# Two convolutions placed anew, and two matrix stages that start on finished tiles

## What is computed

```python
h = rmsnorm_2(x, g_mix[l])
z = h @ w_in[l]
za = z[..., : 2 * D_A] + b_glu[l]
zb = z[..., 2 * D_A: 2 * D_A + D_B]
zc = z[..., 2 * D_A + D_B:]
ua = za[..., :D_A] * jax.nn.sigmoid(za[..., D_A:])
va = causal_dwconv(ua, w_dw_a[l]) + b_dw_a[l]
va = jax.nn.silu(layernorm(va, ln_g_a[l], ln_b_a[l]))
ya = va @ w_a_out[l]
yb = multiscale_pool(zb, w_pool_grp[l], pool_scale[l]) @ w_b_out[l]
gb, gc, xv = zc[..., :D_C], zc[..., D_C: 2 * D_C], zc[..., 2 * D_C:]
yc = (gb * causal_dwconv(gc * xv, w_dw_c[l])) @ w_c_out[l]
gates = jax.nn.sigmoid(h @ w_gate[l] + b_gate[l]).reshape(b, s, N_BRANCH, d)
merged = gates[:, :, 0] * ya + gates[:, :, 1] * yb + gates[:, :, 2] * yc
x = x + merged @ w_o[l]
h2 = rmsnorm_2(x, g_mlp[l])
x = x + jnp.square(jax.nn.relu(h2 @ w_up[l])) @ w_down[l]
```

## Time and profile before

| | us |
|---|---|
| median of 3 runs | 3545.73 |
| lowest, highest | 3545.4, 3550.69 |
| the profiled execution, its own time | 3549.25 |
| its span, first to last instruction | 3547.5 |
| TensorE busy | 3401.6 (96%) |
| VectorE busy | 2297.2 (65%) |
| ScalarE busy | 1234.8 (35%) |
| GpSimd busy | 530.2 (15%) |
| mean granted TensorE clock | 0.979 |

### The profile page before, as it was taken

One profiled execution on the slowest core, in us unless ns is written; L12 is line 12 of the kernel. 1 busy time (PEld: TensorE's weight loads), 2 busy tenths in 40 slices (PEclk: granted clock), 3 DMA queues, 4 the chain that ended last, 5 costly groups with the idle time before them and its releaser, 6 DMA issues.

```text
span 3547.5 us, 71271 instructions
## 1 busy us (share of the span) xinstructions
PE 3401.6 (96%) x31330; PEld 2955.4 (83%) x31330; DVE 2297.2 (65%) x2408; ACT 1234.8 (35%) x1125; POOL 530.2 (15%) x307
## 2 busy tenths in 40 slices
PE   7999799899999999999999998999999999999998
PEld 4777568798888988898889886888888878888887
DVE  7684144699998964796479655449747556564444
ACT  2000142344443334333433333343443334343332
POOL 0374000000354520252035200020000000000000
PEclk8999899999999999999999999999999999999999
DMA  9656594355444555445544553554545545555553
GB/s 412 240 231 278 219 393 168 143 191 202 179 177 180 189 192 209 172 185 199 204 180 180 187 193 140 190 208 172 213 171 197 191 148 195 203 199 190 196 206 119
DMA packets 52019, 713.18 MB, mean 201 GB/s; under 512 B 5690, under 2 KB 7754, under 8 KB 8848
## 3 DMA queue, kind: packets, MB, share of 16 engines
q1 hardware_dynamic: 48528, 700.47, 52.5%
q0 software_dynamic: 1136, 8.17, 0.6%
q10 hardware_dynamic: 2192, 2.10, 0.2%
HBM read 707.04 MB, written 3.67 MB: 200 GB/s over the span
## 4 chain that ended last, share of the span: by engine, by line
PE 87%; DVE 8%; DMA 4%; ACT 1%; issue 1%; DVEq 0%; SPq 0%; ACTq 0%
PE psW L477 24%; PE psW L478 24%; PE psW L479 24%; PE psW L475 6%; DVE ring L982 3%; DMA ring<-wst_dram 3%; DVE arena L1563 2%; PE psM L505 1%; PE psW L545 1%; DMA h_act<-bias_rows 1%; PE psM L699 1%; PE psM L527 1%; PE psM L545 1%; DVE proj L1441 1%; DVE work L1339 1%
## 5 line engine op out<-in xcount | busy, mean ns | idle before, releaser
L982 DVE SCALAR_TENSOR_TENSOR ring<-ring 128x2048 f16<-128x2048 f32 x526 | 1276.7, 2468 | 541.7 <-ACT ring L1688 541.3
L477 PE MATMUL psW<-h_act,ring 128*128 128x256 f16 x5088 | 1391.6, 274 | 49.0 <-DVE h_act L1331 16.6
L478 PE MATMUL psW<-h_act,ring 128*128 128x256 f16 x5088 | 1391.6, 274 | 0.0
L479 PE MATMUL psW<-h_act,ring 128*128 128x256 f16 x5088 | 1391.5, 273 | 0.0
L1688 ACT ACTIVATE ring<-ring 128x2048 f16<-128x2048 f32 x526 | 974.7, 1903 | 862.1 <-PE psW L479 809.2
L477 PE MATMUL psW<-arena,ring 128*128 128x256 f16 x3072 | 841.3, 274 | 8.4 <-DVE arena L1454 4.3
L478 PE MATMUL psW<-arena,ring 128*128 128x256 f16 x3072 | 841.4, 274 | 0.0
L479 PE MATMUL psW<-arena,ring 128*128 128x256 f16 x3072 | 841.2, 274 | 0.0
L477 PEld LDWEIGHTS psW<-h_act,ring 128*128 128x128 f16 x5088 | 498.7, 98 | 125.2 <-issue 40.5
L479 PEld LDWEIGHTS psW<-h_act,ring 128*128 128x128 f16 x5088 | 499.5, 98 | 59.2
L478 PEld LDWEIGHTS psW<-h_act,ring 128*128 128x128 f16 x5088 | 498.9, 98 | 57.9
(11 more groups left out here) (340 smaller groups left out, 2411.9 us busy)
## 6 DMA issues: line engine op xcount, KB each, us to landing
ring<-wst_dram SPq DMA_DIRECT2D x333, 2048.0 KB, 7.8
x_res<-xT_dram POOLq DMA_DIRECT2D x2, 2048.0 KB, 17.4
out_dram<-x_res SPq DMA_DIRECT2D x4, 512.0 KB, 2.6
bias_rows<-proj POOLq DMA_DIRECT2D x1, 1536.0 KB, 21.9
x_res<-cmat_dram POOLq DMA_DIRECT2D x1, 1024.0 KB, 6.7
x_res<-bmat_dram ACTq DMA_DIRECT2D x8, 128.0 KB, 2.6
h_act<-bias_rows ACTq DMA_DIRECT2D x1, 1024.0 KB, 32.2
dyn<-dyn_dram POOLq DMA_DIRECT2D x1, 480.0 KB, 23.6
```

What stands on the lines that cost most here:

```text
L477: nc.tensor.matmul(out, whi(s, col, P), xh, start=first, stop=False)
L478: nc.tensor.matmul(out, whi(s, col, P), xl, start=False, stop=False)
L479: return nc.tensor.matmul(out, wlo(s, col, P), xh, start=False, stop=last)
L982: ins = stt(wlo(s, c, n), ring[:, s * UNIT + c:s * UNIT + c + n], WSCALE, whi(s, c, n), ALU.mult, ALU.subtract)
```

## The change

It does five things.

1. The short convolution becomes a generator of its own, `short_branch()`, and its pieces run ahead of `low` in z's units 11 to 15 (16 is empty).
2. The long convolution yields every two taps, so it takes the pieces 0 to 14 of the gate stage; one empty piece follows, and the layer norm starts at piece 16 as before.
3. Gate uses bank (j + 1) % 4, abc begins with `psM`, w_o uses bank (j + 3) % 4 with `lead=3`, and gate, abc, w_o and down are entered without draining.
4. `merged` is counted up by each abc unit (from 1), and w_o's first unit waits ahead of every second k for the tiles that it reads. The wait of `merge` for VectorE's own last instruction becomes one on `merged`.
5. down starts once `relu_sb` has counted 16 units, and asks for all 32 behind its first unit. The first turn (four units) of w_o and of down is now written out.

```diff
+            from_h1 = lambda s, j: unit_a(s, (j + 1) % 4, h_split)
+            stage("gate", from_h1, n=16, drained=False)
...
-                ps = psW if j % 2 == 0 else psM
+                ps = psM if j % 2 == 0 else psW
...
-            stage("abc", abc, lead=3)
-            pe_.wait_ge(merged, 1)
-            stage("w_o", from_h)
+            stage("abc", abc, lead=3, drained=False)
+            def w_o_head(s, j):
+                for m in range(2):
+                    for k in range(KT):
+                        if m == 0 and k % 2 == 0:
+                            pe_.wait_ge(merged, k // 2 + 2)
+                        mm = product(psW[:, 3, m * T:(m + 1) * T], s, k * 256 + m * P, h_split(k), k == 0, k == KT - 1)
+                return mm
+            stage("w_o", lambda s, j: unit_a(s, (j + 3) % 4, h_split), lead=3, head=w_o_head, drained=False)
...
-            pe_.wait_ge(relu_sb, 32 + 4)
-            stage_sums("down", lambda s, j: unit_b(s, j, lambda k: halves(A, k)), 8)
+            def down_head(s, j):
+                mm = down(s, j)
+                pe_.wait_ge(relu_sb, 4 + 32)
+                return mm
+            pe_.wait_ge(relu_sb, 4 + 16)
+            stage("down", down, n=24, lead=2, drained=False, head=down_head)
...
+            def short_branch():
+                v.wait_ge(bank_free, FIRST["z"] + 9 + 4)
+                step(tt(tiles(J, 6, 6), tiles(J, 6, 6), tiles(J, 12, 6), ALU.mult))
+                for k in range(6):
+                    D.put(ts(tiles(J, 12 + k), tiles(J, 6 + k), const("w_dw_c", 3 * k + 2), None, ALU.mult))
+                yield
...
+                if n >= 11:
+                    next(short)
                 low(FIRST["z"] + n + 2)
...
-                    if tap % 3 == 0:
+                    if tap % 2 == 0:
                         yield
...
-                D.wait()
+                v.wait_ge(merged, i * 4 + (j + 1))
...
-                D.put(tt(hl[:, :, 1, :], w, hl[:, :, 0, :], ALU.subtract))
-            lows("abc", merge, 24)
-            D.wait()
-            v.sem_inc(merged, 1)
+                tt(hl[:, :, 1, :], w, hl[:, :, 0, :], ALU.subtract).then_inc(merged, 1)
+            lows("abc", merge, 20)
```

## The result

| | before | after |
|---|---|---|
| median, lowest to highest (5 runs each) | 3545.73 (3543.44 to 3550.69) | 3527.12 (3521.49 to 3529.23) |
| span of the profiled execution | 3547.5 | 3525.4 |
| mean granted clock | 0.979 | 0.980 |

A forecast was written before the change was run, and what follows sets the result against it. TensorE, busy 96% of the span, was taken as the bound, so only its standstills and slow clock could be won. 1.38 + 7.01 + 1.48 + 6.7 + 6.11 = 22.7 us gave median 3523.0; own range 3519.5 to 3526, full range to 3529.

The forecast's parts named there:

- rival (1): Bare entries to gate, abc, w_o and down cost 1.4 us each, giving back 5.6: 3528.6 us; chance 0.07.
- rival (2): Convolution still paces gate: half of the 7.01 us gained gives 3526.5, none gives 3530.0; chance 0.07.
- z to gate: Gate starts one bank further and waits for older banks only: 1.38 us go.
- Long convolution: In gate, 12 taps and split fit under TensorE's 10.48 us unit; all 7.01 us lost over ten units go.
- Short convolution: Moved to z's units 11 to 15, it costs TensorE nothing; 3.74 us piece at most 8.2 beside GpSimd.
- gate to abc: First abc unit uses psM and waits for the last but one gate unit only: 1.48 us go.
- abc to w_o: w_o starts on units 0 to 6; gap of about 0.5 us stays, gain 6.7 us, bounds 4.9 and 7.2.
- up to down: Down's first unit starts at once: 3.3 us gap and 2.8 us slow clock, all 6.11 us, go.
- Loop entries: Entering gate, abc, w_o and down by or behind a branch, without idle time as cover, costs zero.
- (4): Counting `merged` tile by tile releases w_o no earlier, so abc to w_o gives nothing: 3529.7 us; chance 0.03.
- rival (3): GpSimd beside long convolution slows taps 2.2 times: 4.3 us over per unit, 3588 us, sign turned from seventh unit; chance 0.03.

The follow-up runs named there:

- e5: Changed kernel, but gate and abc are entered drained again: median 3527.58 us, ratio to before 0.9938.
- e1: Changed kernel with both convolutions put back to their earlier places, early starts kept: median 3532.27 us, ratio to before 0.9954.
- e3: Changed kernel, but w_o's first matmul waits for all eight merged units: median 3528.73 us, ratio to before 0.9948.
- e4: Changed kernel, but down's first matmul waits for all 32 squared units: median 3524.84 us, ratio to before 0.9940.
- e8: Changed kernel with idle VectorE work making a longer and a shorter TensorE gap in each of up's eight turns: one execution, 3574.74 us.
- e13: e12 with six small matmuls added ahead of the fourth unit of each of up's turns: one execution, 3569.85 us.
- e11: e4 with six small matmuls (1.3 us, result unused) added between z and gate: one execution, 3529.61 us.
- e2: Kernel before the change with only the convolutions placed as in the change: median 3540.36 us, ratio to before 0.9982.
- e12: Changed kernel with only the longer of e8's two added gaps in each of up's turns: one execution, 3544.75 us.
- e6: Changed kernel, but GpSimd starts its pooling later, beside the long convolution: one execution, 3521.82 us.

## Why the prediction was right

The forecast was 3523.0, within 3519.5 to 3529. The median, 3527.12, is inside that, but 1.1 above the end of the forecast's own range, 3526. By the time alone rival (1) with 3528.6 and half of rival (2) with 3526.5 fit better; it is the trace that rules them out. Against its own execution the sum was 22.7 us of span, and 22.1 were measured. That the total is so close is in part luck, since the two turns of the clock that the sum lacks nearly cancel. The five steps themselves were right, and experiments took each of them back: e5 the two entries, e1 the convolution, e3 the one at w_o and e4 the gap at down. By its steps:

- **z to gate**: 1.38, measured 1.38. It counts only with the convolution: e1 shows that alone it is lost again.
- **Long convolution**: 7.01, measured 7.01; the first split ends at 2401.80 against 2401.7.
- **Short convolution**: nothing, and nothing it cost. Beside GpSimd its pieces are slower as bounded. In the timeline after, product, scalings and six taps:

```profile
2326.05 2.16 DVE L1563 TENSOR_TENSOR proj<-proj 128x1536 f32<-128x1536 f32 x1
2328.25 2.98 DVE L1565 TENSOR_SCALAR proj<-proj,cst 128x256 f32<-128x256 f32 x6
2332.13 4.61 DVE L998 SCALAR_TENSOR_TENSOR ring<-ring 128x2048 f16<-128x2048 f32 x2 [0.90 <-ACT ring L1709]
2336.66 3.40 DVE L1572 SCALAR_TENSOR_TENSOR proj<-proj,cst 128x255 f32<-128x255 f32 x6
...
2348.76 0.74 POOL L2069 TENSOR_TENSOR arena<-work,proj 128x256 f32<-128x256 f32 x1
```

  5.2 us instead of 3.74, under the bound of 8.2; VectorE still waits 0.90 us for ScalarE. GpSimd ends at 2349.5 instead of 2342.8, 200 us before it is asked.
- **gate to abc**: 1.48, measured 1.48.
- **abc to w_o**: 6.7, measured 6.73. One gap of 0.32 by the list (0.49 in the reads) at tile 14, clock 1.00.
- **up to down**: 6.11, measured 6.19.
- **Loop entries**: no gap at any of the four; rival (1) is out. So is (2), with the reads 10.48 us apart through the convolution, and (4), with 6.73 us gained between abc and w_o.
- **A slip in rival (3)**: at 4.3 us a unit the gain of 22.7 is used up with the sixth unit, not the seventh. No conclusion hangs on it.
- **Not in the sum**: 1.67 us lost to the clock at gate's unit 22, which I had written down as "no gain" from its gap and left at 1.00 because the earlier trace rows show 1.00 there; and 1.17 us won in the norm ahead of up. What failed is the step from one row to a rule: a gap of 1.98 us had left the clock alone once, so I took it that it would. e8 and e13 show gaps of 2.3 to 2.4 us that do either. For the gap of 0.5 us the conclusion held, in every trace here.
- **Against the median** the change gained 18.6 us, 3.5 less than in the spans. The two profiled executions differ by 0.14 us up to z's first read. In the fourteen traces, all with the same code up to there, that time varies by 9.5 us, as much as the runs of one kernel differ (7.7 us for after), so it may be most of their spread; the runs without a trace can't show it. Before's profiled execution was 3.5 us above its median and after's is its median. 3.5 us is inside that variation, and I can't ascribe it to a part of the change.

## What to carry to other kernels

A stage boundary costs what its first instruction waits for, so ask which tiles and which bank it needs, not whether the stage before is done. When VectorE feeds TensorE piece by piece, fit each piece under the unit's time; gains on TensorE ahead of a stretch that VectorE paces are taken back there (1.38 us here). Price a gap of 2 us or more as a range, its length and the same with some microseconds of half clock, for moving other code can switch the second on or off.

## What the runs showed of the hardware

- A standstill of TensorE may cost the clock, or not. Where it did, 15 to 28 matmuls followed 0.21 us apart, so 1.2 GHz instead of 2.4 for some 3 to 6 us. These are the gaps behind z's first read, without those in the norm ahead of up, by the list of waits, which counts 0.16 us too little. Those of 1.6 us or less never did (eight in e8). Those of 2.0 to 2.4 us did in some cases and not in others, of the same length in one execution (five and three in e13). Those of 2.9 us did not (e4, e11), while those of 3.2 (e2) and those of 5.0 (e3, granted clock 0.52 behind it), 5.2 and 5.3 (e2) did. The price was 1.7 to 2.8 us.
- The Trainium skill (TensorE: Matmul & The Clock Gate, Part 1) says that the chip judges activity in windows that run freely of the kernel. The mixture in e13 agrees. By itself that does not explain why the gap at gate's unit 22 cost the clock in each of the seven traces in which it lies at the same distance from z's first read (e12 and e13 among them), and in none of the five with another distance. That distance is 404.8 us in the seven and 406.2 or 413.2 in the five, while the executions reached z at times up to 9.5 us apart. Here the outcome went with the place in the program and not with the execution; what ties the two was not tried.
- A VectorE tap beside GpSimd took 0.56 us instead of 0.39 (e6), and GpSimd's pooling 34 us instead of 23, 7.33 of them its first copy. The pair of sizes in the earlier trace rows (2.2 times) is for another operation and was no guide to this one.
